# Differential attention of a two-block transformer kernel: the score products, maxima and exponentials of neighbouring units issued half a unit apart

## The reference, cut to what matters

```python
def diff_attend(q, k, v, lam, g_subln, lam_init):
    s = jnp.einsum('bqhcd,bkhcd->bchqk', q, k) * ATTN_SCALE      # c = 0, 1; ATTN_SCALE = 1/8
    p = jax.nn.softmax(s, axis=-1)
    w = p[:, 0] - lam * p[:, 1]
    o = jnp.einsum('bhqk,bkhd->bqhd', w, v)
    o = o * lax.rsqrt(jnp.mean(o * o, axis=-1, keepdims=True) + EPS) * g_subln
    return (o * (1.0 - lam_init)).astype(v.dtype)
```

## Time and profile before

| | us |
|---|---|
| median of 3 runs | 3775.08 (3772.36 to 3781.18) |
| the profiled execution, its time | 3779.68 |
| its span in the trace | 3777.8 |
| PE busy in the span | 3460.0 (92%) |
| DVE busy | 1653.2 (44%) |
| ACT busy | 1445.5 (38%) |
| POOL busy | 1189.3 (31%) |
| TensorE clock granted over the span, share of full | 0.96 |

### The profile page before, as it was taken

How to read it: one execution, slowest core, us unless ns; L and a number is a source line. 1 busy time by engine, 2 the same in 40 slices (tenths; PEclk the granted TensorE clock), 3 DMA queues, 4 the chain that set the end, 5 groups by cost and what they waited for, 6 DMA issues and landing times. The chain is left out here.

```text
span 3777.8 us, 44046 instructions
## 1 busy us (share of the span) xinstructions
PE 3460.0 (92%) x17208; PEld 2662.6 (70%) x17208; DVE 1653.2 (44%) x2274; ACT 1445.5 (38%) x1791; POOL 1189.3 (31%) x555
## 2 busy tenths in 40 slices
PE   7999897789959999999728999999999999899999
PEld 5975586568736666666427777777788878678887
DVE  4136525730156666666644444444432131453212
ACT  4225432252234555555234444443432233343221
POOL 3410022644302333333114333322134443233443
PEclk9999998999979999999869999999999999999999
DMA  5312110012227999999722222222032221013222
GB/s 221 100 68 79 67 66 24 1 67 89 89 94 253 345 350 346 360 367 371 300 79 92 73 79 73 73 64 93 24 112 101 93 86 67 23 67 112 97 92 78
DMA packets 94480, 494.53 MB, mean 131 GB/s; under 512 B 21647, under 2 KB 21903, under 8 KB 43761
## 3 DMA queue, kind: packets, MB, share of 16 engines
q1 hardware_dynamic: 74496, 452.75, 33.6%
q0 software_dynamic: 19824, 39.54, 2.9%
HBM read 470.18 MB, written 40.89 MB: 135 GB/s over the span
## 5 line engine op out<-in xcount | busy, mean ns | idle before, releaser
L272 PE MATMUL ps<-arena_r,arena_r 128*128 128x512 f32 x2080 | 828.1, 398 | 39.7 <-POOL ring_r L263 25.0
L273 PE MATMUL ps<-arena_r,arena_r 128*128 128x512 f32 x2080 | 816.2, 392 | 0.0
L263 POOL TENSOR_TENSOR ring_r<-ring,arena_r 128x2048 fp32r<-128x2048 f32 x100 | 465.8, 4659 | 842.7 <-ACT arena_r L259 842.7
L259 ACT ACTIVATE arena_r<-ring 128x2048 fp32r<-128x2048 f32 x166 | 316.7, 1909 | 489.2 <-PE ps L274 335.1
L272 PEld LDWEIGHTS ps<-arena_r,arena_r 128*128 128x128 f32 x2080 | 393.8, 189 | 137.3 <-issue 43.9
L273 PEld LDWEIGHTS ps<-arena_r,arena_r 128*128 128x128 f32 x2080 | 394.3, 190 | 81.7 <-issue 1.9
L263 POOL TENSOR_TENSOR arena_r<-ring,arena_r 128x2048 fp32r<-128x2048 f32 x66 | 304.1, 4608 | 414.3 <-ACT arena_r L259 414.3
L274 PE MATMUL ps<-arena_r,arena_r 128*128 128x512 f32 x1056 | 410.8, 389 | 0.0
L274 PE MATMUL ps<-arena_r,ring_r 128*128 128x512 f32 x1024 | 404.3, 395 | 0.0
L1949 DVE TENSOR_TENSOR arena_r<-arena,arena_r 128x2048 fp32r<-128x2048 f32 x132 | 301.9, 2288 | 170.3 <-ACT arena_r L1907 170.1
L1907 ACT ACTIVATE arena_r<-arena 128x2048 fp32r<-128x2048 f32 x132 | 250.9, 1910 | 130.2 <-DMA arena<-we_gu 107.2
(11 more groups left out here) (397 smaller groups left out, 6015.1 us busy)
## 6 DMA issues: line engine op xcount, KB each, us to landing
ring<-wstream SPq DMA_DIRECT2D x193, 1024.0 KB, 4.9
arena<-we_gu SPq DMA_DIRECT2D x132, 1024.0 KB, 8.1
arena<-we_down SPq DMA_DIRECT2D x66, 1024.0 KB, 7.6
arena<-ys SPq DMA_DIRECT2D x32, 512.0 KB, 8.5
arena<-arena SPq DMA_DIRECT2D x192, 64.0 KB, 2.0
arena<-arena SPq DMA_DIRECT2D x32, 128.0 KB, 4.3
arena<-x_t SPq DMA_DIRECT2D x1, 2048.0 KB, 14.2
h<-arena SPq DMA_DIRECT2D x1, 2048.0 KB, 6.6
```

The source lines that it names most:

```text
L259: act.activation(whalf(c, 0), ring[:, c % NSLOT, :], ACT.Copy).then_inc(sem("chunk_hi"), 1)
L263: pool.tensor_tensor(whalf(c, 1), ring[:, c % NSLOT, :], whalf(c, 0).bitcast(F32), ALU.subtract).then_inc(sem("chunk_lo"), 1)
L272: pe.matmul(out, hi, rhs[0], start=start, stop=False)
L273: pe.matmul(out, hi, rhs[1], start=False, stop=False)
```

## The change

The functions that write a unit's scores, maxima and exponentials now take one component, and the three lists are interleaved anew. No instruction is added or removed, and no buffer changes.

```diff
@@ da_tensor @@
-            def scores(n):
+            def scores(n, c):
                 h, qt = divmod(n, TT)
-                for c in range(2):
-                    if n >= 1:
-                        pe.wait_ge(sem("da_exp"), 2 * (n - 1) + c + 1)
...
-            scores(0)
+            scores(0, 0)
+            scores(0, 1)
+            scores(1, 0)
             for n in range(NU):
                 if n + 1 < NU:
-                    scores(n + 1)
+                    scores(n + 1, 1)
+                if n + 2 < NU:
+                    scores(n + 2, 0)
                 turn(n)
@@ da_vector @@
-            for n in range(NU + 1):
-                if n >= 1:
-                    diff(n - 1)
-                if n < NU:
-                    row_max(n)
-                if n < KT:
-                    QX.rebuild(dve, n)
-                if n % 4 == 3 and n > 4:
-                    head(n // 4 - 1)
+            row_max(0, 0)
+            row_max(0, 1)
+            QX.rebuild(dve, 0)
+            for n in range(NU):
+                if n + 1 < NU:
+                    row_max(n + 1, 0)
+                diff(n)
+                if n + 1 < NU:
+                    row_max(n + 1, 1)
+                if n + 1 < KT:
+                    QX.rebuild(dve, n + 1)
+                if n % 4 == 2 and n > 4:
+                    head(n // 4 - 1)
@@ da_scalar @@
+            def exponent(n, c):
+                s = SC[:, 16 * (n % 2):16 * (n % 2) + 16]
+                act.wait_ge(sem("da_bias"), 2 * n + c + 1)
+                if n >= 2:
+                    act.wait_ge(sem("da_turn"), n - 1)
+                act.activation(prob(n, c), pf[:, 1024 * c:1024 * c + TA], ACT.Exp, scale=0.125,
+                               bias=s[:, 2 + c:3 + c], accum_out=s[:, 4 + c:5 + c]).then_inc(sem("da_exp"), 1)
+
+            exponent(0, 0)
             for n in range(NU):
...
+                exponent(n, 1)
+                if n + 1 < NU:
+                    exponent(n + 1, 0)
                 if n >= 1:
                     turned(n - 1)
```

More of the change, by code:

```diff
@@ L701, in da_tensor @@
         def da_tensor(pe):
-            def scores(n):
+            def scores(n, c):
                 h, qt = divmod(n, TT)
-                for c in range(2):
-                    if n >= 1:
-                        pe.wait_ge(sem("da_exp"), 2 * (n - 1) + c + 1)
[L707 to L710, removed]
+                if n >= 1:
+                    pe.wait_ge(sem("da_exp"), 2 * (n - 1) + c + 1)
+                q = Q[64 * c:64 * c + 64, h, qt * P:qt * P + P]
+                pe.matmul(bank(2 * c), q, K[64 * c:64 * c + 64, h, 0:512], start=True, stop=True)
+                pe.matmul(bank(2 * c + 1, 256), q, K[64 * c:64 * c + 64, h, 512:TA], start=True,
+                          stop=True).then_inc(sem("da_scores"), 1)
             def mod_turn(n):
@@ L759, in da_vector, with row_max @@
         def da_vector(dve):
-            def row_max(n):
+            def row_max(n, c):
                 s = SC[:, 16 * (n % 2):16 * (n % 2) + 16]
[L762 to L767, removed]
+                dve.wait_ge(sem("da_scores"), 2 * n + c + 1)
+                dve.reduce_max(s[:, c:c + 1], pf[:, 1024 * c:1024 * c + TA], AX.X).then_inc(sem("da_max"), 1)
+                dve.wait_ge(sem("da_max"), 2 * n + c + 1)
+                dve.tensor_scalar(s[:, 2 + c:3 + c], s[:, c:c + 1], -0.125, None,
+                                  ALU.mult).then_inc(sem("da_bias"), 1)
             def diff(n):
@@ L820, in rstd @@
                 act.activation(view(SQ + 512, 512), view(SQ + 512, 512), ACT.Exp, scale=-0.5).then_inc(sem("da_rstd"), 1)
-            for n in range(NU):
[L823 to L829, removed]
+            def exponent(n, c):
[6 more added lines that the diff above has]
+            exponent(0, 0)
+            for n in range(NU):
+                exponent(n, 1)
+                if n + 1 < NU:
+                    exponent(n + 1, 0)
                 if n >= 1:
```

## The result

| | before | changed |
|---|---|---|
| median, us | 3780.67 (7 runs, 3772.36 to 3791.39) | 3803.75 (7 runs, 3795.03 to 3813.55) |
| profiled execution, its time | 3779.68 | 3813.55 |
| stage of the attention, first scores to the next stage's first line 296 | 215.1 | 231.8 |
| a group of four units | 24.90 | 26.57 |

The ratio is 1.0053, with a 95% interval of 1.0037 to 1.0068: 20 us slower (14 to 26). The same kernel measured again beside 30 runs of before gave 1.0048 (1.0030 to 1.0065), 18 us. The time lies 14 us above the 3789.9 that was predicted, and above 3799, the end of the range.

The account below looks back on a forecast made before the run. TensorE was taken as the bound, its scores' late component waiting for VectorE's chain. Start 3.0, units 2 to 4 1.7, groups 9.3 and tail 0.8 made 14.8 us, on median 3775.08 giving 3789.9; range 3780 to 3799.

Parts of the forecast that it names:

- The scores cost 1.49 from the later component's start: TensorE's scores in each unit: 1.49 us from the later component's start, whatever the head start of the other.
- E(n+1,0) waits for X(n-1), and S(n+2,0) for it: Each unit: component 0's exponential waits for transposes that read its buffer, and TensorE's next component 0 scores wait for it.
- 1.14 in a plain unit, 0.28 behind Q, 0 behind V: Delay of the second scores on TensorE by unit type; a group loses 2.56 instead of 1.08, 1.48 more.
- The distances of line 723: Expected spacing of TensorE's modulation product: 5.6, 5.6, about 10.7 and 5.3 to 4.7, rather than 4.86, 5.12, 9.60, 5.31.
- The sum, 14.8: Attention stage: start 3.0, units 2 to 4 1.7, six groups with unit 7 9.3, tail 0.8; together 14.8 us more.
- the 0.4 for unit 7: Where rebuilding and the head's product meet on VectorE in unit 6, a maximum comes about 0.4 late, and unit 7 too.
- the third round: Stage start: a further scores round ahead of unit 0's turning product, moving its modulation product from 245.65 to 249.1.
- the last term: Stage end, units 29 to 31: the last component 0 exponential ahead of the next stage's rounding delays the tail by 0.8.
- a component alone is cheap: Rival listed first: each scores component alone needs much less than 1.49; change +0.9, 3776; 0.08 shared with strict order.
- the wait is over in time: Rival: the second scores' wait for the exponential ends in time, TensorE never stalls; 3769.5; chance 0.04.
- the low stretches that were to give 3800: Clock rival: three more half-clock stretches inside the stage, 3.4 us each, give 3800; chance 0.08.
- strict order: Rival: TensorE's matmuls start strictly in list order, so the 1.14 delay costs 0.18; 3780.6; 0.08 shared with cheap components.

Follow-up runs that it names:

- e6: Changed kernel with the scores of component 0, two units ahead, moved behind the modulation product, ahead of the transposes; ratio 1.0157, group 32.30.
- e3: Changed kernel with a third buffer for component 0's exponentials, so their wait for transposes reaches one unit further back; ratio 1.0019, group 24.98.
- e4: Changed kernel with V's six products issued in pairs behind units 0, 1, 2 of the next head, Q behind unit 3; ratio 0.9996, group 24.16.
- e1: Changed kernel measured again with no edit; ratio 1.0048, stage 233.8, group 26.57.
- e10: Repeat run of the kernel before with V's products spread in pairs over three units and the head's product between VectorE's maxima; ratio 0.9976, group 23.82.
- e8: Changed kernel with VectorE's difference put back ahead of both maxima, TensorE and ScalarE still staggered; ratio 1.0163, group 32.79.

## Why the prediction was wrong, and what of it held

The time missed. The direction and the mechanism held, point by point; the step that failed stands behind them.

- *The scores cost 1.49 from the later component's start.* 1.48 in the unit at 346.30, and e6 shows 1.48 to 1.50 for a component alone. That a pair takes no longer agrees with the Trainium skill (TensorEngine Tiling (Array Packing), Key Properties), by which different tiles of the array work independently and in parallel. The strict program order of matmuls that the Trainium skill (TensorE: Matmul & The Clock Gate, The mechanism) states did not come back in any run: pairs started together in the changed kernel, too.
- *E(n+1,0) waits for X(n-1), and S(n+2,0) for it.* Shown by the releasers of the changed kernel, by e3 (the buffer takes 1.6 of the 1.67 away) and by e4 (cover takes it away with the wait in place).
- *1.14 in a plain unit, 0.28 behind Q, 0 behind V.* It was 1.22, 0.35 and 0. The term was small by 0.07 because the exponential started 0.17 after the unit and not 0.10; I had taken the step from the end of transposes to ScalarE from the copy W. In the rows of the changed kernel (345.08, 345.25) it is 0.07 more for the exponential; why was not tried. A group came out at 26.55 to 26.68, near the 26.4 predicted. The distances of line 723 that I had listed beside it, about 10.7 and 5.3 to 4.7, don't follow from these terms: with 0 behind V that unit had to stay at 9.60, as it did, and the one behind transposes at 5.65.
- *The sum, 14.8.* The stage grew by 16.7, by its own parts: up to unit 1's product 2.4 (3.0 was predicted; 4.5 in e1, near the 4.6 that I had given for a clock that stays low), units 2 to 4 1.9 (1.7), the six groups 10.0 (9.3 with the 0.4 for unit 7, of which 0.13 came), behind unit 28's product 2.4 (0.8). The 2.4 at the start is near the 3.0 partly by luck: the third round, which I had put wholly at the lower clock, ran at the higher one, and unit 0's product came 1.7 later than before and not 3.5; then the clock fell on that product, which I had let rise. Of the last term, the delay of X(31) is 0.8 as predicted; the other 1.6 is the last V at the lower clock for longer: 8.40 for its 12 records in the changed kernel, where it took 6.80 before. Nothing in my sum stood for a clock at the end of the stage.
- *The rivals.* That a component alone is cheap is refuted by e6. That the wait is over in time is refuted by the rows above. The clock did not fall inside the stage: it was at the higher level through all steady units, with half the array in use for most of the scores. So the low stretches that were to give 3800 are not what put the time above the range. The changed kernel's busy times from 253.74 to 458.54 (the clock again behind POOL):

```profile
253.74:458.54 204.80, 200.36 (x1081) 119.28 (x1079) 129.55 (x251) 100.61 (x206) 4.50 (x1) 1.00 0.24 82
```

For strict order I had added 2.9 and 2.65 to the time before and got 3780.6, but left out the 8.2 that the stagger would give back, which I did subtract for the first rival. With it that rival stands at 3772.4, below the range that was to take it in.

**The step that failed is the conversion to a time.** I added 14.8 to the median of three runs, 3775.08, and let the range end at 3799. The median of before was 3780.67 over seven runs, and 3786.1, 3785.0 and 3786.6 over the 30, 23 and 22 runs of three later comparisons. Those were on three chips, and the chip of the first runs isn't on record, so whether three runs were too few or the chip was another stays open. I had noted that the three runs lay 9 us apart and still took their middle as if it stood firm; the range held the difference, with a few us for the clock, and hardly anything for the base. With the base of the 30 runs the sum gives 3801, and the changed kernel's medians were 3803.75 and 3802.57.

The base alone isn't all, though. Of the 13.9 us between 3789.9 and 3803.75, the seven runs' base accounts for 5.6 and the stage, 16.7 instead of 14.8, for 1.9; the other 6.4 lie outside the stage. There the sum had nothing ("the later stages only move"), and the range had no room for their scatter. That this is scatter is likely but not proven: in e1 the ratio gives 18 us for a stage that is 18.7 longer, and over all eleven comparisons the time's change by the ratio less the stage's change is between -3 and +6 us. The 20 and 18 us contain the stage's 17 within their intervals.

**Where the 34 us of the two profiles lie.** 2.4 came before the stage, 16.7 in it, 14.8 behind it. Half of the last is in one place. Busy times in the changed kernel from 2653 to 2684, and below them those of the kernel before over the same work:

```profile
2653.00:2684.00 31.00, 26.57 (x91) 19.27 (x90) 12.98 (x16) 10.81 (x14) 9.01 (x2) 0.51 0.01 4
```

```profile
2631.40:2654.95 23.55, 20.30 (x90) 14.67 (x90) 10.22 (x16) 10.65 (x14) 9.38 (x2) 0.68 0.00 1
```

The same products took 31.0 us at a mean clock of 0.51 and 23.6 at 0.68, in a stage that the change doesn't touch; the lower clock is there in both, but for longer in one. The other profiles bear on whether that is chance: the time behind the stage was 3324.6 before, 3339.4 and 3329.1 in the two profiles of the changed kernel, and 3314.6 to 3339.1 in the nine others, with 270 to 310 us at the lower clock. The longest but one belongs to e10, whose stage is 8 us shorter than before. The stage's length doesn't order these times. But before has only one profile, and it has the least time at the lower clock; that the change shifts the mean behind the stage by a few us, as e3's interval could suggest, stays open.

## What to carry to other kernels

When a loop is staggered so that one chain gets shorter, look for waits that were always over before: a buffer's release that had half a unit of slack lands on the path once its user moves ahead, and it costs the whole round of the engines that it passes through. Where a group has one unit with much independent work and several with none, spread that work over the units before any order is changed: here it removed the old stall without the stagger, and with the same few lines it covered the stagger's own round but for 0.34 us in a group. And price a change against as many runs of the kernel before as can be had: a sum that is right to 2 us is worth little on a base that three runs fix to 10. A range for the time needs room for the scatter of the whole program as well as for the mechanism.

## What was not expected of the hardware

- Two f32 products on different halves of the array's rows take the same time together as one alone (1.49 in a pair, 1.48 to 1.50 alone), and the second half's 512 columns start with the first's (four weight loads together at 330.29), although the first half's 256 columns stand ahead of them in the list and start only at 331.25, 0.96 later.
- Within the changed kernel's stage the lower clock cost only what lay at its edges, though half the array was idle in most scores between them. The same V took 5.32 in the middle of the stage, 6.80 at the end before and 8.40 in the changed kernel, and the start of the stage varied by 2 us between two executions of one kernel. In e6 and e8, whose TensorE waited in most units, it came inside the stage too.
- The time behind the stage, in which every kernel has the same instructions, varied by 25 us over twelve profiles.
